# Totals of the norms in PSUM banks, a block-by-block tail of each section's first three blocks, and an early first decay in an fp32 model of 512 tokens

## What is computed

```
for layer in range(2):
    hf = swiglu(rms(x, g[0]), w_gate[0], w_up[0], w_down[0]);  x = x + 0.5 * rms(hf, g[1])
    xn = rms(x, g[2])
    mix = attn_mixer(xn) if layer == 0 else mlstm_mixer(xn);   x = x + rms(mix, g[3])
    hf = swiglu(rms(x, g[4]), w_gate[1], w_up[1], w_down[1]);  x = x + 0.5 * rms(hf, g[5])
```

## Time and profile before

| | |
|---|---|
| median of 3 runs | 2593.22 us (2593.08 to 2597.55) |
| the profiled execution, its own time | 2594.58 us |
| its span | 2592.8 us |
| mean granted TensorE clock | 0.987 |
| busy: PE, DVE, ACT, POOL | 2491.6, 1040.2, 984.8, 1294.6 us |
| chain that ended last: PE, issue, DVE, POOL, DMA, ACT | 70%, 10%, 8%, 7%, 3%, 3% |

### The profile page before, as it was taken

The page is one execution under the profiler, slowest core; times in us unless marked ns, Lnnn a source line. Parts: engine busy times, 40 slices in busy tenths (PEclk is TensorE's granted clock), DMA queues, the critical chain, the costliest instruction groups (busy, mean ns, idle before and its releaser), DMA issues.

```text
span 2592.8 us, 31087 instructions
## 1 busy us (share of the span) xinstructions
PE 2491.6 (96%) x11446; PEld 2012.7 (78%) x11446; DVE 1040.2 (40%) x1488; ACT 984.8 (38%) x1325; POOL 1294.6 (50%) x681
## 2 busy tenths in 40 slices
PE   8999999999899999999999999998999998998997
PEld 6888887856788888888888778687888887877676
DVE  3222322145722212322241650545222692724885
ACT  5333333366433333433333333434333433233553
POOL 5555455400465554655544544236555554246873
PEclk9999999999999999999999999999999999999999
DMA  4333442200233333233333223012333444333751
GB/s 139 96 97 97 146 129 90 89 17 1 65 106 97 97 98 108 87 97 95 94 104 104 75 87 98 17 49 82 97 97 97 146 154 163 107 90 88 185 133 65
DMA packets 79995, 251.68 MB, mean 97 GB/s; under 512 B 9731, under 2 KB 14211, under 8 KB 79788
## 3 DMA queue, kind: packets, MB, share of 16 engines
q1 hardware_dynamic: 72384, 235.55, 30.0%
q10 hardware_dynamic: 6684, 11.90, 1.5%
q0 software_dynamic: 848, 3.15, 0.4%
HBM read 237.54 MB, written 15.25 MB: 97 GB/s over the span
## 4 chain that ended last, share of the span: by engine, by line
PE 70%; issue 10%; DVE 8%; POOL 7%; DMA 3%; ACT 3%; SPq 0%; POOLq 0%; DVEq 0%; ACTq 0%
PE banks L1837 19%; PE banks L1838 18%; PE banks L1839 18%; POOL wl_sb L385 5%; DMA raw_sb<-weights 2%; PE banks L1903 2%; PE banks L1904 2%; PE banks L1909 2%; DVE mix_sb L2204 1%; POOL xl_sb L416 1%; PE banks L1783 1%; PE banks L657 1%; PE banks L1790 1%; PE banks L885 1%; PE banks L894 1%
## 5 line engine op out<-in xcount | busy, mean ns | idle before, releaser
L385 POOL TENSOR_TENSOR wl_sb<-raw_sb,wh_sb 128x1024 fp32r<-128x1024 f32 x401 | 974.0, 2431 | 976.4 <-ACT wh_sb L377 973.6
L1837 PE MATMUL banks<-xh_sb,wh_sb 128*128 128x512 f32 x2016 | 790.0, 392 | 17.0 <-POOL wl_sb L385 17.0
L1838 PE MATMUL banks<-xh_sb,wl_sb 128*128 128x512 f32 x2016 | 786.1, 390 | 0.0
L1839 PE MATMUL banks<-xl_sb,wh_sb 128*128 128x512 f32 x2016 | 785.8, 390 | 0.0
L377 ACT ACTIVATE wh_sb<-raw_sb 128x1024 fp32r<-128x1024 f32 x401 | 424.9, 1060 | 781.2 <-DMA raw_sb<-weights 767.7
L1837 PEld LDWEIGHTS banks<-xh_sb,wh_sb 128*128 128x128 f32 x2016 | 379.2, 188 | 108.0 <-POOL wl_sb L385 15.3
L1839 PEld LDWEIGHTS banks<-xl_sb,wh_sb 128*128 128x128 f32 x2016 | 379.1, 188 | 79.2
L1838 PEld LDWEIGHTS banks<-xh_sb,wl_sb 128*128 128x128 f32 x2016 | 379.3, 188 | 77.9 <-issue 0.2
L1837 PE MATMUL banks<-hh_sb,wh_sb 128*128 128x512 f32 x704 | 274.1, 389 | 0.2 <-POOL wl_sb L385 0.2
L1838 PE MATMUL banks<-hh_sb,wl_sb 128*128 128x512 f32 x704 | 274.0, 389 | 0.0
L1839 PE MATMUL banks<-hl_sb,wh_sb 128*128 128x512 f32 x704 | 274.0, 389 | 0.0
(11 more groups left out here) (368 smaller groups left out, 2693.9 us busy)
## 6 DMA issues: line engine op xcount, KB each, us to landing
raw_sb<-weights SPq DMA_DIRECT2D x404, 512.0 KB, 3.6
park<-xs_sb ACTq DMA_DIRECT2D x12, 512.0 KB, 3.6
mix_sb<-scratch SPq DMA_DIRECT2D x16, 258.0 KB, 5.7
hf_sb<-scratch SPq DMA_DIRECT2D x16, 258.0 KB, 5.1
mix_sb<-park SPq DMA_DIRECT2D x4, 1024.0 KB, 7.1
scratch<-scratch ACTq DMA_DIRECT2D x1, 2560.0 KB, 12.1
scratch<-mix_sb SPq DMA_DIRECT2D x8, 259.5 KB, 2.9
x_sb<-x_in SPq DMA_DIRECT2D x8, 256.0 KB, 8.5
```

Of the source, the lines that this page charges most:

```text
L385: pool.tensor_tensor(wl[:, slot, :], raw[:, slot, :], wh_f[:, slot, :], ALU.subtract).then_inc(w_split, 1)
L1837: pe.matmul(dst, wh[:, q, cols], in_hi, start=first, stop=False)
L1838: pe.matmul(dst, wl[:, q, cols], in_hi, start=False, stop=False)
L1839: return pe.matmul(dst, wh[:, q, cols], in_lo, start=False, stop=last)
```

## The change

It has three parts.

**Totals.** The running totals of chunks 1 to 5 are kept in banks 6, 5 and 4 in place of SBUF; the add of chunk 6 reads the bank and writes the total to SBUF, from where `col_sum` reads it as before. Of each of the adds of chunks 2 to 6 one input is now a bank; those of chunk 1 read two slots in SBUF and write a bank.

**Tail.** In the first three blocks of a section the last chunk is made block by block, three matmuls of `product3` a block, and `blocks_done` is raised after each. In `attention_out` the last two chunks (3 and 7) are, in `memory_out` chunk 7.

**First decay.** POOL copies `ms_sel` behind the split of the gates, before its low parts of mlstm.qk. PE spreads head 0's row between blocks 4 and 5 of mlstm.o, into bank 7 (`first_spread`), DVE reads it there, and ACT makes the decays of head 0 after the sigmoid of block 5. The loop over the o blocks on ACT is written out.

```
-            pe.wait_ge(g_cols, 2)
             pe.wait_ge(tiles_freed, FREE0 + TILE["mlstm.o"] + 8)
-            spread_m(0)
             for u in range(HEADS + 2):
...
-            evac(act, "mlstm.o", 8, lambda i, m: act.activation(at(sigo, 4 * i + m), lin[m], ACT.Sigmoid))
+            for b in range(8):
+                high_part(act, "mlstm.o", b % 4, b - b % 4)
+                act.wait_ge(blocks_done, BLK["mlstm.o"] + b + 1)
+                act.activation(sigo[:, b, :], lin[b % 4], ACT.Sigmoid).then_inc(tiles_freed, 1)
+                if b == 5:
+                    decays(0)
...
+            def three_last(ks):
+                for s in range(3):
+                    for k in ks:
+                        last = product3(pe, lin[s], s, k, xh[:, k, :], xl[:, k, :], False, k == ks[-1])
+                    last.then_inc(blocks_done, 1)
 
             def first_three(name, key):
 
                 pe.wait_ge(tiles_freed, FREE0 + TILE[name])
-                for k in range(KD + 1):
-                    if k < KD:
-                        if key in DEFERRED:
-                            pe.wait_ge(x_high, X_HIGH[key] + k + 1)
-                        else:
-                            pe.wait_ge(hi_ready, SPLIT[key] + k + 1)
+                for k in range(KD):
+                    if key in DEFERRED:
+                        pe.wait_ge(x_high, X_HIGH[key] + k + 1)
+                    else:
+                        pe.wait_ge(hi_ready, SPLIT[key] + k + 1)
+                    if k < KD - 1:
                         three_high(name, k, k == 0)
                     if k:
                         pe.wait_ge(xn_ready, SPLIT[key] + k)
-                        three_low(k - 1, k == KD)
...
+                        three_low(k - 1)
+                pe.wait_ge(xn_ready, SPLIT[key] + KD)
+                three_last((KD - 1,))
+
+            def attention_out():
+                for chunk in (0, 1, 2, 4, 5, 6):
+                    pe.wait_ge(a_oev if chunk < 4 else a_oev2, chunk % 4 + 1)
+                    three_high("attn.out", chunk, chunk == 0)
+                    three_low(chunk)
+                pe.wait_ge(a_oev, 4)
+                pe.wait_ge(a_oev2, 4)
+                three_last((3, 7))
...
@@ -2024,6 +2042,8 @@
+                if b == 4:
+                    first_spread(pe)
@@ -2200,9 +2220,9 @@
                         for w, slots in enumerate((S0, SG, SP)):
                             if m > 1:
                                 dve.wait_ge(acc_ready, ADDED[name] + 3 * (m - 2) + w + 1)
-                            total = buf[:, TOTAL[w], :]
-                            dve.tensor_tensor(total, buf[:, slots[0], :] if m == 1 else total, buf[:, slots[m % 2], :],
-                                              ALU.add).then_inc(acc_ready, 1)
+                            kept = banks[:, TOTAL_BANK[w], :]
+                            dve.tensor_tensor(buf[:, TOTAL[w], :] if m == KD - 2 else kept, buf[:, slots[m % 2], :],
+                                              buf[:, slots[0], :] if m == 1 else kept, ALU.add).then_inc(acc_ready, 1)
```

More of the change, by code:

```diff
@@ L870, in gate_columns_tensor, with first_spread @@
             last.then_inc(g_pe, 1)
+        def first_spread(pe):
+            pe.wait_ge(m_staged, 1)
+            pe.wait_ge(g_cols, 2)
+            pe.matmul(ps_n, ms_sel[:, 0, :], m_row, start=True, stop=True).then_inc(m_mb, 1)
         def mlstm_tensor(pe, memory_out):
             def spread_m(u):
[L875 to L878 removed]
+                pe.wait_ge(m_dm, u)
                 pe.matmul(banks[:, 3, :], ms_sel[:, u, :], m_row, start=True, stop=True).then_inc(m_mb, 1)
@@ L1060, in distances @@
                 for s in range(4):
-                    last = ts(packed(dm[u % 3], s), banks[:, 3, P * s:T], ccols[:, s, u:u + 1], 0.0,
+                    last = ts(packed(dm[u % 3], s), banks[:, 3 if u else 7, P * s:T], ccols[:, s, u:u + 1], 0.0,
                               ALU.subtract, ALU.max)
@@ L1773, in odd_vector @@
             residual(dve, "odd.out", "final")
-        wide_sums = [banks[:, 6, :], banks[:, 5, :], banks[:, 4, :]]
+        TOTAL_BANK = (6, 5, 4)
+        wide_sums = [banks[:, bank, :] for bank in TOTAL_BANK]
         sums = [w[:, 0:T:P] for w in wide_sums]
@@ L1924, in first_three @@
                         pe.wait_ge(xn_ready, SPLIT[key] + k)
-                        three_low(k - 1, k == KD)
-            def attention_out(chunk):
-                pe.wait_ge(a_oev if chunk < 4 else a_oev2, chunk % 4 + 1)
-                three_high("attn.out", chunk, chunk == 0)
-                three_low(chunk, chunk == KD - 1)
+                        three_low(k - 1)
[9 more added lines that the diff above has]
+                three_last((3, 7))
             def memory_out(chunk):
                 pe.wait_ge(m_hh, chunk + 1)
-                three_high("mlstm.out", chunk, chunk == 0)
+                if chunk < KD - 1:
+                    three_high("mlstm.out", chunk, chunk == 0)
                 pe.wait_ge(m_hid, chunk + 1)
-                three_low(chunk, chunk == KD - 1)
+                if chunk < KD - 1:
+                    three_low(chunk)
+                else:
+                    three_last((chunk,))
             def linear(name, key=None, amid=None, begun=False):
@@ L2008, in _ @@
             pe.wait_ge(tiles_freed, FREE0 + TILE["attn.out"])
-            for chunk in (0, 1, 2, 4, 5, 6, 3, 7):
-                attention_out(chunk)
+            attention_out()
             linear("attn.out", begun=True)
```

16 lines of the change are left out of this document (4 added, 12 removed).

## The result

The changed kernel takes 2567.47 us (median of 4 runs, 2563.67 to 2570.88); before, in the same runs, 2595.39 us (2593.08 to 2599.09). The ratio is 0.9891, 95% interval 0.9870 to 0.9912, so 28.3 us less, between 23 and 34. The prediction of 2565 us and its range of 2559 to 2577 hold. The profiled execution took 2565.56 us, 29.0 less than that of before.

What follows compares the result with a forecast made beforehand. TensorE, busy 96% of the span, was taken as the bound, so only fewer stalls or a better clock help. Terms 19.6 + 1.0 + 2.8 + 4.8 = 28.2 us gave 2565.0 us, range 2559 to 2577.

Steps and rivals of the forecast that it cites:

- Part A, 19.6 + 1.0: Totals in banks: both stalls and their clock echo in attn.out and mlstm.out go, 19.6 us; 1.0 more in ffn3.dn.
- Part B, +6.6: Block-by-block tail: block 0's slot is freed earlier, shortening stalls in front of block 4 in seven sections, 6.6 us gained.
- Part B, -3.8: Block-by-block tail where x is split late (attn.qk, ffn1 to ffn3): nine matmuls stand behind the last xl, 3.8 us lost.
- Part C, +4.8: Start of the mLSTM heads: head 1's products 6.1 us earlier, less 1.3 for the moved spread, 4.8 us gained.
- 1 (half of A): attn.out and mlstm.out: the lag is not made up, half the totals' gain is left, 2575.3 us; chance 0.08.
- 2 (the change does not do what it says): Bank-operand adds are held as well, or their wait was for something else; 7.6 us gained, 2585.6 us; chance 0.04.
- 3 (the clock falls ahead of the nine matmuls): Four late-split sections: idle time the tail adds lowers the clock, 2.1 to 2.9 us each, 2575.4 us; chance 0.06.
- 4 (adds in banks above 1.59 us): attn.out and mlstm.out: adds reading and writing banks cost more than 1.59 us each, kernel slower; 2608 us at 2.0; chance 0.02.

Runs made afterwards that it cites:

- A alone: Only the running totals moved to banks, the rest as in the kernel before; ratio 0.9912, 2573.32 us.
- C alone: Only the first decay moved among the o blocks, the rest as in the kernel before; run twice, ratios 0.9969 and 0.9973.
- the copy alone: Only the selector copy on GpSimd made early, the rest as in the kernel before; ratio 0.9975.
- the one with two SBUF inputs: Changed kernel, but the adds of chunks 2 to 5 add a chunk's SBUF slot to itself, output still in the bank; ratio 0.9949, 2580.64 us.
- B alone: Only the block-by-block tail, the rest as in the kernel before; run twice, ratios 0.9978 and 0.9984.

## Why the prediction was right

- **The bound.** "Nothing but fewer PE stalls, or PE work at a better clock": PE's busy time fell by 4.9 us, the span by 29.0.
- **Part A, 19.6 + 1.0.** Measured 9.4 + 10.2 = 19.6, to the tenth, and 1.7 in ffn3.dn for 1.0, of which 0.2 stand in front of block 4 and are counted under part B, so 1.5. The bound of 1.3 was too low: PE's wait of 1.34 us went, and the eight matmuls behind it fell from 1.16 to 1.06 us (`2113.15 1.06 PE L1795`, no idle time before it). The price of an add, 0.69 to 0.75 us, was 0.68 to 0.70. The first trio stayed at 4.11 us, as taken; ACT waited 3.98 us for it, and then never again in that stage. The margin of "about 1 us" in the last block is 0.7. The argument that decided was the pair of rows in one trace, one operand in a bank and no spread, two in SBUF and up to four times as long.
- **Part B, +6.6.** The stalls in front of block 4 fell by 0.88 (mlstm.qk), 0.66 (mlstm.out), 1.05 (even.out), 0.91 (odd.in), 0.93 (odd.out) and 0.79 (even.in), and attn.out's 1.44 with its restart by 1.7: 6.9 in all. Even.in's 0.79 can't be put down to the tail: there the stall was 3.0 to 3.2 us without it in A alone, C alone (twice) and the copy alone, 3.0 to 4.1 with a tail of one chunk, and 4.44 in before. And from odd.pre to the last spread, where odd.in and odd.out should give 1.8, the changed kernel is only 0.8 us shorter than before; in that stretch 14 profiles lie between 217.3 and 222.8 us, with the tail (217.3 to 222.8) and without it (219.9 to 222.2).
- **Part B, -3.8.** Measured 0.3 in attn.qk, 1.1, 0.8 and 0.9 in ffn1 to ffn3 once block 4 has given some back: -3.1. The working, nine matmuls behind xl(7), is in the lines above; the idle of about a microsecond that was to stand in front of them came as three of 0.39, 0.37 and 0.22 us.
- **Part C, +4.8.** Head 1's products are 5.0 us earlier. The copy was named as the first link; that it is worth 4.2 of the 5 was not said.
- **The sum, and luck.** The terms as measured make 19.6 + 1.5 + 6.9 - 3.1 + 5.0 = 29.9 us, against 29.0 between the profiled executions. Between the two stand steps that no part made: 1.4 us gained in the attention heads, and 0.7 lost by the end of ffn0, 1.05 at the start of mlstm.qk and 1.0 of part B's gain behind odd.pre. They nearly cancel in this pair of profiles and need not in another. The interval of the result is 23 to 34 us less, so that forecast, profile and medians agree within 1 us is luck; what the runs bear out is the terms, but for even.in's.
- **The rivals.** 1 (half of A) is out: A alone is 22.9 us. 2 (the change does not do what it says) is out by the same run, and its mechanism by the one with two SBUF inputs. 3 (the clock falls ahead of the nine matmuls) is out: B alone is not slower, the steps behind the tail are 1.1 to 1.3 us and not 3 to 4, the idle times are 0.2 to 0.4 us. 4 (adds in banks above 1.59 us) is out: 0.70 at most.

What was missed: part B's cost in the late sections was worked out at 3.8 us and left standing as part of a net gain. It could have been read as a better kernel, with the tail only where it pays.

## What to carry to other kernels

Where VectorE and GpSimd both work from SBUF, look at the spread of one instruction's duration: a minimum of 0.68 and a maximum of 2.90 us for the same form pointed to a neighbour here, and an operand in an idle PSUM bank took it away without a change of the arithmetic. Price a stall with its echo in the clock (here 2.1 to 2.9 us behind 7.3), and look at what stands last in a helper engine's queue: a copy of 1 us that depends on nothing belonged at the first idle time. A reordering that frees a buffer early paid only where its inputs were early; sort the call sites by that before applying it to all.
